# Stick-breaking attention: decay scans of two neighbouring units joined into 1024 columns in one in-place ring, and the diagonal mask added on TensorE

## The reference

```python
for blk in range(S // Q_BLOCK):              # 128 queries a block
    t0 = blk * Q_BLOCK; t1 = t0 + Q_BLOCK
    z = jnp.einsum('bthd,bshd->bhts', qb, kb)          # q scaled by d ** -0.5
    strict = jnp.arange(t1)[None, :] < jnp.arange(t0, t1)[:, None]
    log_beta = jax.nn.log_sigmoid(z)
    log_keep = jnp.where(strict, jax.nn.log_sigmoid(-z), 0.0)
    after = lax.cumsum(log_keep, axis=3, reverse=True) - log_keep
    A = jnp.where(strict, jnp.exp(log_beta + after), 0.0)
    outs.append(jnp.einsum('bhts,bshd->bthd', A, vb))
```

## Time and profile before

| | |
|---|---|
| median of 3 runs | 3419.16 us (3419.09 to 3419.75) |
| the profiled execution | 3420.38 us, its span 3418.6 us |
| PE busy over the span | 3246.3 us (95%) |
| DVE busy | 2486.0 us (73%) |
| ACT busy | 1925.7 us (56%) |
| POOL busy | 705.0 us (21%) |
| the scans of the attention (L1481) | 1152, from 1582.56 to 2887 us |

### The profile page before, as it was taken

One profiled execution on the slowest core, in us unless ns is written; L12 is line 12 of the kernel. 1 busy time (PEld: TensorE's weight loads), 2 busy tenths in 40 slices (PEclk: granted clock), 3 DMA queues, 4 the chain that ended last, 5 costly groups with the idle time before them and its releaser, 6 DMA issues. The chain is left out here.

```text
span 3418.6 us, 74728 instructions
## 1 busy us (share of the span) xinstructions
PE 3246.3 (95%) x28402; PEld 2670.1 (78%) x28402; DVE 2486.0 (73%) x3501; ACT 1925.7 (56%) x4177; POOL 705.0 (21%) x677
## 2 busy tenths in 40 slices
PE   6998999999999999997999999999999998999998
PEld 4776888999999988886666666666666666888887
DVE  4775445443578893326999999999999998666665
ACT  4553122222333452225888888888888887555554
POOL 1323333200000003421112221311131113232322
PEclk9999999999999999998999999999999999999999
DMA  8989778977955579974011201211111013566664
GB/s 293 331 316 322 268 258 298 305 239 237 321 162 185 186 245 320 320 262 139 21 39 58 63 28 31 64 65 31 40 57 53 11 33 91 183 205 199 200 204 135
DMA packets 415615, 582.77 MB, mean 170 GB/s; under 512 B 35568, under 2 KB 298096, under 8 KB 414288
## 3 DMA queue, kind: packets, MB, share of 16 engines
q1 hardware_dynamic: 394560, 506.56, 44.9%
q0 software_dynamic: 16960, 58.73, 5.1%
q10 hardware_dynamic: 3792, 13.30, 1.0%
HBM read 393.74 MB, written 184.75 MB: 169 GB/s over the span
## 5 line engine op out<-in xcount | busy, mean ns | idle before, releaser
L1481 DVE TENSOR_TENSOR_SCAN a_prod<-a_keep,a_prod,a_zeros 128x512 f32<-128x512 f32 x896 | 1067.7, 1265 | 3.0 <-ACT a_keep L1405 1.8
L1419 ACT COPY a_turned<-a_rt 128x512 f32<-128x512 f32 x960 | 529.8, 622 | 170.4 <-PE a_rt L1332 169.9
L1405 ACT ACTIVATE a_keep<-a_z 128x512 f32<-128x512 f32 (+3 forms) x1152 | 561.4, 596 | 1.5 <-PE a_z L1317 1.5
L1345 PE MATMUL a_acc<-a_turned,c_dw 128*64 128x256 f32 x4352 | 520.7, 380 | 2.5 <-ACT a_osum L1429 2.5
L1332 PEld LDWEIGHTS a_rt<-c_ident,a_prod 64*128 64x128 f32 x8448 | 328.4, 139 | 236.5 <-DVE a_prod L1481 175.2
L1332 PE MATMUL a_rt<-c_ident,a_prod 64*128 64x64 f32 x8448 | 369.0, 226 | 94.8 <-DVE a_prod L1481 62.3
L1345 PEld LDWEIGHTS a_acc<-a_turned,c_dw 128*64 128x64 f32 x4352 | 287.5, 137 | 147.6 <-ACT a_turned L1417 10.3
L1317 PE MATMUL a_z<-c_khi,a_q 64*128 64x512 f32 (+3 forms) x2304 | 369.3, 397 | 14.0 <-DMA c_dw<-scratch_dw 12.5
L1293 POOL TENSOR_SCALAR_AFFINE_SELECT a_keep<-a_keep 128x256 f32<-128x256 f32 x128 | 128.6, 1017 | 1045.5 <-ACT a_keep L1405 1045.0
L939 DVE TENSOR_TENSOR p_hlo<-p_wraw,p_hlo 128x1024 fp32r<-128x1024 f32 x85 | 104.4, 1228 | 323.6 <-ACT p_hlo L704 323.6
L704 ACT CAST p_hlo<-p_wraw 128x1024 fp32r<-128x1024 f32 x85 | 89.1, 1049 | 392.0 <-PE p_bank L572 210.4
(11 more groups left out here) (299 smaller groups left out, 6353.0 us busy)
## 6 DMA issues: line engine op xcount, KB each, us to landing
p_hlo<-scratch_parts SPq DMA_DIRECT2D x130, 512.0 KB, 5.0
p_wraw<-scratch_sums SPq DMA_DIRECT2D x128, 512.0 KB, 6.7
p_aslot<-scratch_parts SPq DMA_DIRECT2D x62, 512.0 KB, 5.1
p_u<-in_w_in POOLq DMA_DIRECT2D x64, 256.0 KB, 5.8
scratch_wsums<-p_u POOLq DMA_DIRECT2D x32, 512.0 KB, 6.7
p_hraw<-scratch_sbv POOLq DMA_DIRECT2D x32, 512.0 KB, 7.4
m_xt<-in_x SPq DMA_DIRECT2D x32, 512.0 KB, 5.1
out_y<-c_pair SPq DMA_DIRECT2D x32, 512.0 KB, 4.4
```

Source lines behind the costliest of these rows:

```text
L1345: last = pe.matmul(acc[h * SD:(h + 1) * SD, lo:QW], dw[:, h, j * TPC + kb, :], turned[:, (FIRST[u] + kb // 2) % TB, kb % 2, h * QW + lo:(h ...
L1405: act.activation(keep[:, at % KB, 0:w], z[at % ZB][:, 0:w], ACT.Sigmoid, scale=-Z_SCALE).then_inc(keep_done, 1)
L1419: act.copy(dst, src).then_inc(turned_done, 1)
L1481: dve.tensor_tensor_scan(prod[:, u % PB, s, 0:w][:, ::-1], keep[:, at % KB, 0:w][:, ::-1], zeros[:, 0:w], first, ALU.mult, ALU.add).then_i ...
```

## The change

- Units of a row are taken in pairs (`PAIRS`), two neighbours in each, and one alone at the end of a row with an odd number. A head pair has 40: 32 of two units and 8 of one; in all 160, of which 32 have one unit. `keep` and `prod` become one `ring` with three slots of four strips by 1024 columns. ACT writes its sigmoids into the slot (the earlier unit in the upper half), DVE scans it in place, and PE transposes out of it. `gates` waits until the pair three before is transposed.
- A strip of a pair is one scan of up to 1024 columns: 640 scans in place of 1152. It waits for the sigmoids of the pair's last unit. Its second operand is one column of `zeros`, read again and again, instead of 512 zeros.
- `turn` waits for the four scans of the pair. PE and ACT run two pairs ahead: `ahead` holds the units of pair p + 2, one is issued with each unit of pair p, and what is left with the last.
- POOL's mask is gone. PE adds -2^60 to the scores on and above the diagonal instead, with one more matmul of 128 columns on each strip of a diagonal unit (256 in all): the sigmoid of that is 1. POOL makes its operands `eye` and `shut` once, at the stage's start.
- Tiles of the stage's opening (`ig`, `fg`, `mlast` and others) now lie in the tile `pair`, so SP's first loads of `wout_raw` and `wgate`, which go there too, wait until POOL has read them.

```diff
+    PAIRS, PAIR_OF = [], []
+    for row in range(len(LAST)):
+        for u in range(LAST[row - 1] + 1 if row else 0, LAST[row] + 1, 2):
+            PAIRS.append(range(u, min(u + 2, LAST[row] + 1)))
+            PAIR_OF += [len(PAIRS) - 1] * len(PAIRS[-1])
+
+    def place(u):
+        return PAIR_OF[u] % RP, 1 - (u - PAIRS[PAIR_OF[u]][0])
...
-        keep = sb("keep", [P, KB, CH])
-        prod = sb("prod", [P, PB, 4, CH])
+        ring = sb("ring", [P, RP, 4, 2, CH])
         turned = sb("turned", [P, TB, 2, CH])
-        zeros = sb("zeros", [P, CH])
+        zeros = sb("zeros", [P, P])
+        eye, shut = sb("eye", [P, P], F32R), sb("shut", [P, P], F32R)
...
+            sp.wait_ge(g_const, 6)
+            sp.dma_start(d["m"].rearrange("h (c t) -> (h c) t", t=P), m[:]).then_inc(m_out, 16)
+            sp.wait_ge(g_const, 7)
+            sp.wait_ge(m_out, 16)
             sp.dma_start(wout_raw, w_out[0:P, :]).then_inc(wout_in, 16)
             sp.dma_start(wgate, w_ada[0:P, 2 * D:3 * D]).then_inc(wgate_in, 16)
-            sp.wait_ge(g_const, 6)
-            sp.dma_start(d["m"].rearrange("h (c t) -> (h c) t", t=P), m[:]).then_inc(m_out, 16)
...
-                for i in range(2):
-                    w, at = width(u, i), (4 * u + 2 * i) % KB
-                    tail = keep[:, at:at + 2, w - P:w]
-                    pool.wait_ge(keep_done, 4 * u + 2 * i + 2)
-                    pool.affine_select(out=tail, in_=tail, compare_op=ALU.is_gt, fill=1.0, base=0,
-                                       pattern=[[0, 2], [-1, P]], channel_multiplier=1).then_inc(mask_done, 1)
+                pool.wait_ge(keep_done, 4 * u + 4)
...
+                    if diag(u):
+                        pe.wait_ge(shut_done, 3)
+                        for h in range(2):
+                            pe.matmul(z[(at + h) % ZB][:, w - P:w], eye[:], shut[:], start=False, stop=True, skip_group_check=True).then_inc(z_done, 1)
...
-                pe.wait_ge(scan_done, 4 * u + 4)
+                slot, part = place(u)
+                pe.wait_ge(scan_done, 4 * PAIR_OF[u] + 4)
...
-            for u in range(NU):
-                turn(u, 0)
-                if u + 2 < NU:
-                    scores(u + 2)
-                if blocks(u) > 2:
-                    turn(u, 1)
-                if u:
-                    weigh(u - 1)
+            for p, pair_units in enumerate(PAIRS):
+                ahead = list(PAIRS[p + 2]) if p + 2 < len(PAIRS) else []
+                for u in pair_units:
+                    turn(u, 0)
+                    if ahead:
+                        scores(ahead.pop(0))
+                    if blocks(u) > 2:
+                        turn(u, 1)
+                    if u == pair_units[-1] and ahead:
+                        scores(ahead.pop(0))
+                    if u:
+                        weigh(u - 1)
...
             def gates(u):
+                slot, part = place(u)
+                if PAIR_OF[u] >= RP:
+                    act.wait_ge(rt_done, FIRST[PAIRS[PAIR_OF[u] - RP][-1] + 1])
...
-            for u in range(NU):
+            for p, pair_units in enumerate(PAIRS):
                 for s in range(4):
-                    at, i, w = 4 * u + s, s // 2, width(u, s // 2)
-                    if diag(u):
-                        dve.wait_ge(mask_done, 2 * UNITS[u][1] + i + 1)
+                    head, i = pair_units[0], s // 2
+                    run = slice(0 if len(pair_units) == 2 else CH, CH + width(head, i))
+                    n = run.stop - run.start
+                    dve.wait_ge(keep_done, 4 * pair_units[-1] + s + 1)
+                    if diag(head):
                         first = 1.0
                     else:
-                        dve.wait_ge(keep_done, at + 1)
-                        dve.wait_ge(scan_done, at + 1 - 4)
-                        first = prod[:, (u - 1) % PB, s, 0:1]
-                    if u >= PB:
-                        dve.wait_ge(rt_done, FIRST[u - PB + 1])
-                    dve.tensor_tensor_scan(prod[:, u % PB, s, 0:w][:, ::-1], keep[:, at % KB, 0:w][:, ::-1], zeros[:, 0:w],
-                                           first, ALU.mult, ALU.add).then_inc(scan_done, 1)
+                        dve.wait_ge(scan_done, 4 * p + s + 1 - 4)
+                        first = ring[:, (p - 1) % RP, s, 0, 0:1]
+                    line = ring[:, p % RP, s].rearrange("p a t -> p (a t)")[:, run][:, ::-1]
+                    dve.tensor_tensor_scan(line, line, zeros[:, 0:1].to_broadcast([P, n]), first, ALU.mult, ALU.add).then_inc(scan_done, 1)
```

More of the change, by code:

```diff
@@ L24 @@
 BIG = 1.0e30
+SHUT = -2.0 ** 60
 C_QK, C_V, C_O, C_Z, C_G = 0, 1024, 1536, 2048, 2560
@@ L1331, in turn @@
                                 rows = slice(half * HB, (half + 1) * HB)
-                                last = pe.transpose(rt[(2 * k + half) % RB][:, at:at + HB], prod[rows, u % PB, 2 * i + h, kb * P:(kb + 1) * P], ident[rows, rows])
+                                last = pe.transpose(rt[(2 * k + half) % RB][:, at:at + HB], ring[rows, slot, 2 * i + h, part, kb * P:(kb + 1) * P], ident[rows, rows])
                 last.then_inc(rt_done, 1)
@@ L1403, in gates @@
                     act.wait_ge(z_done, at + 1)
[L1404 to L1405 removed]
+                    act.activation(ring[:, slot, s, part, 0:w], z[at % ZB][:, 0:w], ACT.Sigmoid, scale=-Z_SCALE).then_inc(keep_done, 1)
             def copies(u, pair):
```

52 lines of the change are left out of this document (34 added, 18 removed).

## The result

The changed kernel takes 3462.9 us (median of 4 runs, 3460.41 to 3465.65) against 3419.45 for the kernel before on the same chip: a ratio of 1.0125, 95% interval 1.0114 to 1.0137. It is slower by 43 us, and lies outside the range that was given (3364 to 3428).

The account below looks back on a forecast made before the run. DVE's queue of scans was taken to bound the attention stage, with PE and ACT close behind. Joined scans -56, POOL's mask gone -23, PE's mask and pair waits +54, the start +2 made -23 us: 3396 us, range 3364 to 3428.

Parts of the forecast that it names:

- term 3: Mask matmuls on PE: 0.5 us a diagonal unit, 32 us in all, a third on the path, 10 us more.
- term 4: DVE waiting for both units' sigmoids in pairs: 46 + 8 + 12 - 22 = 44 us more.
- term 2: Mask leaves POOL: DVE's waits and stretched scans beside 128 masks go, 23 us less.
- Term 1: Joined scans on DVE: 512 fewer fixed parts of 0.110 us, 56 us less; 1024-column scans 2.24 us apart.
- no change: Rival: a scan's fixed part is saved by half, or a column costs 2% more; 3421 to 3424 us, 13%.
- full single: Full unit alone at a row's end: DVE waits 1.9 us behind it, 24 of them, 46 us.
- chain of 6.6 us: From a pair's transposes to the sigmoids of the second unit two pairs ahead: 4.4 + 2.2 = 6.6 us.
- short heads: Pairs whose head has 128 and 256 columns: some 0.7 us wait each, a dozen not behind singles, 8 us.
- ends of head pairs: Two single diagonal units with 5.7 us of scans end a head pair: about 4 us wait, three times, 12 us.
- The rest: First scan waits for the second unit's sigmoid, 2 us more; POOL's operands and SP's later loads cost nothing.
- Slower: Rival: PE becomes the bound through masks of 1.45 us a diagonal unit, 60% on the path; 3442 us, 14%.
- The waits are small: Rival: ACT catches up in the pairs or mask matmuls hide, some 10 of 54 us left; 3352 us, 17%.

Follow-up runs that it names:

- Run 2: The changed kernel with the mask matmuls left out and no mask anywhere: 3419.2 us (ratio 0.9997).
- run 5: The kernel before with POOL's mask left out, so no mask at all: 3401.0 us (ratio 0.9945).
- run 6: The changed kernel with each mask matmul on PE issued twice: 3492.6 us (ratio 1.0215).
- run 3: The changed kernel with the mask back on POOL, applied to the ring, none on PE: 3419.7 us (ratio 1.0000).
- run 15: The changed kernel with two matmuls for each score in place of three (product with the queries' low part left out): 3447.4 us (ratio 1.0083).

## Why the prediction was wrong

The forecast was 3396 us and the time is 3462.9: 67 us. Run 2 cuts this in two. Without term 3 the forecast would have been 3386 us, and the kernel with no mask takes 3419.2. So 33 us of the miss are there without any mask, and 34 are PE's mask. Of the 33, some 20 are waits (term 4), 8 the tail and 4 term 2.

**Term 1, joined scans: right.** Scans of 1024 columns are 2.24 us apart, so 512 x 0.110 = 56 us are saved; by the distances it was 55. That settles the weighing against the Trainium skill (VectorE: DVE Perf Modes, the TRN2 errata). Its advice to use large tiles holds here; its 58 cycles of fixed cost, which gave an estimated 31 us, are too few for this scan. The rival *no change*, which had half of the fixed part saved, fell with it.

**Term 2, the mask leaves POOL: right within 4 us.** 19 us by run 5, 23 predicted. That a further 22 us of stretched scans would disappear in the new waits held as well. By the distances of the scans, what DVE takes beyond its count was 68.6 us before and is 50.9 in run 5. In the changed kernel it is 28.6, outside the places in the table: 56 + 40 = 96 us less, for 101 forecast. (DVE's busy time fell by 84.4 only, because 9.0 of the 68.6 us were idle time already, and some 3 us of the new waits lie under the end of a scan's record.)

**Term 3, the mask on PE: wrong in share and in size.** This is the step that failed. It was put at 0.5 us a diagonal unit, 32 us, and a third of it on the path, 10 us. The traces show 0.79 and 1.01 us a unit, 58 us, and three quarters of it on the path, 43.7 us. The share weighs more. PE's load was compared with DVE's over a unit, 0.25 us of room in 4.7, and a third taken, whereas the head's masks stand in the chain that term 4 had already shown to end last. At a third, 58 us would have been 19. The size was taken from matmuls among others of their kind, 0.11 to 0.12 us each, which run 6 bears out (0.11); the 0.14 us a group and the longer scores in front of the groups were not in it. Masks of over 0.6 us are also one of the signs of being wrong that the prediction named, if it meant a diagonal unit's four.

**Term 4, what the pairs cost: the mechanism held, places and sizes did not.** A full single was to cost 1.9 us. Without masks it costs 49.1 / 24 = 2.05, so that part was right. With them it is 3.4: the masks were counted on PE but not put into the chain of 6.6 us, and that a pair's step begins when its scans end, which the 6.6 us take for granted, doesn't hold in the half of the places where PE is still at `weigh` (2022.31 to 2024.19). Of the 20 short heads in the table, the twelve whose row does not follow a single unit were taken at 8 us and have 8.5 without masks. But behind the other eight DVE waits as well, 1.3 us each, 10.5 us that the prediction left out. The ends of head pairs were taken at 12 and have 18.9 without masks, 27 with them. Full pairs behind full pairs wait for nothing, as said. In all the waits are 127.5 us against the 76 of terms 3 and 4; without masks 85 against 66.

**The rest.** The start was to be 2 us later. Counted from the last matmul of the projections it is 2.0 later with no mask and 3.5 with PE's; the 2.8 in front of that are spread. The tail was taken as nothing and is 7.7 us: DVE's wait for PE there went from 10.5 to 18.4. With no mask it is 18.4 too, and with one unit a pair 12.1, so it belongs to the pairs. That the last pair's units come free together fits, but was not tested.

**The sum as it came out**, from the views: DVE's work -84.4, its idle time +115.7, start +6.3, what follows +7.7, so +45.3 us of span. The forecast had -101, +76 and +2. By the distances it is -96 and +128 for the stage, with the same start and tail: the savings came nearly as forecast, and the waits did not.

**The rivals.** *Slower* was the case that came. It had 3442 us through masks of 1.45 us a unit, 60% on the path; they are 0.90 and three quarters on it. Its condition, from 0.6 us a unit on the path, is what the runs show (0.68). Its reason, that PE becomes the bound, holds only for the chain: with 105 us less to do PE gives back 15.5. Even its 3442 is 21 us short, for want of the waits without masks and the tail. *The waits are small* fell: it rested on ACT and PE catching up, and runs 2, 3 and 15 show 68 to 108 us of waits when they have the room.

**What stays open.** Why a mask group takes 0.14 us beside its matmuls, and why the scores of 512 columns in front of it take 0.19 more: a change between half and full array fits, but no run has mask matmuls on half the array. What makes PE late in the twelve places in front of short heads was not followed back. Nor is it shown why four slots with PE's mask keep 85.0 us of waits, 40 of them behind the short heads.

## What to carry to other kernels

When operations of two units are joined, the unit of hand-over doubles too. Before costing it, follow the chain from the joined operation's end to the next one's last input in the trace, with everything that the in-order engines have queued in between, and compare it with the shortest piece of work that must cover it; the mean load of each engine doesn't tell this. Work put on a nearly full engine is priced by its place: the same masks take PE 58 us in both schedules, and cost 14.5 us in one and 43.7 in the other; 105 us of matmuls taken from elsewhere gave back 15.5. A saving that only fills a wait is not to be added: POOL's masks cost 19 us without pairs and 0.5 with them. And when a change makes the granularity coarser, the order of the look-ahead has to be looked at with it, and the depth of the ring. With POOL's mask the even order alone made the joined scans worth 14 us in the ring of the change (3406.1), the fastest here that computes all of the reference. With a fourth slot it was 30 (3389.4), but for that slot this kernel has no room as it stands. A deeper ring without the order gave nothing where it was tried, with PE's mask.

## What the runs showed of the hardware

- A scan with a pointer start costs 0.110 us beside its columns at 512 and at 1024 columns alike (1.175 and 2.243 us apart), at 512 in place or not, and with a repeated zero column as the second operand or a full tensor.
- Two fp32 mask matmuls on the full array, 128 columns each, put between score matmuls on half the array take 0.37 us, four take 0.59: 0.11 us each and 0.14 a group. Two in bf16 take 0.22.
- Six score matmuls in front of such a group take up to 0.19 us more than with no group behind them (0.89 for 0.70 with 512 columns), and with 256 columns 0.05 less. A diagonal unit's masks so take PE 0.79 or 1.01 us, with pairs and without.
- POOL's masks, 128 instructions recorded with 127.6 us, cost DVE 19 us in the kernel before. With pairs they cost 0.5 us (runs 2 and 3), and there DVE has waits in which such a loss can disappear. That this is the reason was not shown apart.
